# The widest probability tile of each attention step is scaled on ScalarE instead of VectorE

## The reference

```python
# fox, for each head and block of 128 queries
s = einsum('bhqd,bhkd->bhqk', qi, k) * SCALE + ci[..., None] - c[:, :, None, :]
p = masked_softmax(s, kpos[None, :] <= qpos[:, None])
o = einsum('bhqk,bkhd->bqhd', p, v)
# nsa, three such attentions (cmp, slc, win), each with a bias from a table of distances
out = sum(sigmoid(gate_logit)[..., None] * stack([o_cmp, o_slc, o_win], -2), axis=3)
```

## Time and profile before

| | us |
|---|---|
| median of 3 runs | 1925.82 |
| lowest, highest | 1923.39, 1929.86 |
| the profiled execution, its own time | 1926.27 |
| its span, first to last instruction | 1924.5 |
| busy in the span: PE, DVE, ACT | 1701.3, 1176.1, 733.3 |
| the first attention's 32 steps | from about 195 to 432 |

### The profile page before, as it was taken

How to read it: one execution, slowest core, us unless ns; L and a number is a source line. 1 busy time by engine, 2 the same in 40 slices (tenths; PEclk the granted TensorE clock), 3 DMA queues, 4 the chain that set the end, 5 groups by cost and what they waited for, 6 DMA issues and landing times.

```text
span 1924.5 us, 22173 instructions
## 1 busy us (share of the span) xinstructions
PE 1701.3 (88%) x7666; PEld 1357.5 (71%) x7666; DVE 1176.1 (61%) x1751; ACT 733.3 (38%) x1215; POOL 142.9 (7%) x162
## 2 busy tenths in 40 slices
PE   7988889989869999999779785989898699999995
PEld 5867766668747777777647553778677578888884
DVE  6465788876475565655463597778875555344354
ACT  5234766554333222222142233553332354233232
POOL 0002300000000000000200492000000000000000
PEclk9988999999979999999589797999999899999998
DMA  4236811112424444443111110002222123223232
GB/s 151 90 117 175 159 53 58 60 34 77 174 90 173 153 162 154 154 163 120 44 44 66 44 55 11 1 1 88 79 85 77 66 88 98 88 99 98 96 100 77
DMA packets 46982, 178.96 MB, mean 93 GB/s; under 512 B 6256, under 2 KB 6512, under 8 KB 44608
## 3 DMA queue, kind: packets, MB, share of 16 engines
q1 hardware_dynamic: 38304, 136.75, 21.4%
q0 software_dynamic: 8608, 41.29, 7.0%
HBM read 168.04 MB, written 4.73 MB: 90 GB/s over the span
## 4 chain that ended last, share of the span: by engine, by line
PE 56%; DVE 23%; ACT 5%; issue 5%; DMA 1%; DVEq 1%; ACTq 0%; SPq 0%
PE ps L1603 15%; PE ps L1604 14%; PE ps L1605 14%; DVE conv L1489 3%; PE ps L1864 1%; DVE rstd L1427 1%; DVE sq_acc L942 1%; DVE mod_a L1304 1%; DVE pt_lo L1452 1%; PE ps L1806 1%; DVE w_lo L931 1%; PE ps L1767 1%; PE ps L1808 1%; PE ps L1807 1%; ACT w_hi L528 1%
## 5 line engine op out<-in xcount | busy, mean ns | idle before, releaser
L1603 PE MATMUL ps<-h_hi,w_hi 128*128 128x512 f32 x1216 | 493.7, 406 | 80.2 <-DVE f_lo L1322 17.3
L1604 PE MATMUL ps<-h_lo,w_hi 128*128 128x512 f32 x1216 | 482.1, 396 | 0.0
L1605 PE MATMUL ps<-h_hi,w_lo 128*128 128x512 f32 x1216 | 481.4, 396 | 0.0
L1603 PEld LDWEIGHTS ps<-h_hi,w_hi 128*128 128x128 f32 x1216 | 233.6, 192 | 153.8 <-issue 58.6
L528 ACT ACTIVATE w_hi<-raw 128x1024 fp32r<-128x1024 f32 x198 | 208.2, 1052 | 269.3 <-DMA raw<-in_panels 262.0
L931 DVE TENSOR_TENSOR w_lo<-raw,w_hi 128x1024 fp32r<-128x1024 f32 x205 | 255.1, 1244 | 78.4 <-ACT w_hi L528 59.2
L1605 PEld LDWEIGHTS ps<-h_hi,w_lo 128*128 128x128 f32 x1216 | 233.4, 192 | 50.4
L1604 PEld LDWEIGHTS ps<-h_lo,w_hi 128*128 128x128 f32 x1216 | 234.0, 192 | 49.3 <-issue 2.9
L1605 PE MATMUL ps<-f_hi,w_lo 128*128 128x512 f32 x432 | 170.6, 395 | 0.0
L1603 PE MATMUL ps<-f_hi,w_hi 128*128 128x512 f32 x432 | 170.6, 395 | 0.0
L1604 PE MATMUL ps<-f_lo,w_hi 128*128 128x512 f32 x432 | 170.6, 395 | 0.0
(11 more groups left out here) (355 smaller groups left out, 2677.4 us busy)
## 6 DMA issues: line engine op xcount, KB each, us to landing
raw<-in_panels SPq DMA_DIRECT2D x252, 512.0 KB, 3.5
wm<-in_w_mod POOLq DMA_DIRECT2D x16, 1536.0 KB, 10.0
scratch_r<-r POOLq DMA_DIRECT2D x8, 320.0 KB, 9.4
X<-in_x SPq DMA_DIRECT2D x4, 512.0 KB, 7.7
bias<-scratch_c POOLq DMA_DIRECT2D x8, 256.0 KB, 9.1
kd<-k_hi POOLq DMA_DIRECT2D x16, 128.0 KB, 3.7
kd<-k_lo POOLq DMA_DIRECT2D x16, 128.0 KB, 5.3
bias<-scratch_r POOLq DMA_DIRECT2D x8, 256.0 KB, 2.9
```

The source lines that it names most:

```text
L1603: pe.matmul(out, w_hi[:, u, b, :], hi[:, k, :N], start=start, stop=False)
L1604: pe.matmul(out, w_hi[:, u, b, :], lo[:, k, :N], start=False, stop=False)
L1605: ins = pe.matmul(out, w_lo[:, u, b, :], hi[:, k, :N], start=False, stop=stop)
```

## The change

The multiplication of the widest tile (t = 3, 128x512) moves from DVE to ACT for the 24 steps that are fox, slc or win. DVE raises a new semaphore `factor_ready` when the factors are there, then scales three tiles (four small ones in a `cmp` step). ACT, in turn `s` behind its last `hi_turn` and ahead of the panel, the head and the bias, waits for `factor_ready` (in every turn, `cmp` too), and scales the widest tile of step `s-1`. PE's turn 0 now waits for `normed` and for `wide_normed`.

```diff
@@ scalar
+        def wide_normed(s):
+
+            if not 0 <= s < NI:
+                return
+            act.wait_ge(sem("factor_ready"), s + 1)
+            if is_big(s):
+                buf, w = scores_of(s, NT - 1)
+                f = (factor if inst[s][0] == "fox" else factor2)[:, s % 3, NT - 1:NT]
+                act.activation(buf, buf, ACT.Copy, scale=f).then_inc(sem("wide_normed"), 1)
...
             hi_turn(s - 2, 2)
             hi_turn(s - 2, 3)
+            wide_normed(s - 1)
             for g in gates_ended(s):
                 panel_hi(BASE["gate"] + g + AHEAD)
@@ vector
-            for t in range(NT):
+            dve.sem_inc(sem("factor_ready"), 1)
+            for t in range(NT if kind == "cmp" else NT - 1):
                 buf, w = scores_of(s, t)
                 last = dve.tensor_scalar(buf, buf, f[:, t:t + 1], None, ALU.mult)
             last.then_inc(sem("normed"), 1)
@@ tensor
             if j == 0:
                 pe.wait_ge(sem("normed"), s + 1)
+                pe.wait_ge(sem("wide_normed"), sum(is_big(r) for r in range(s + 1)))
```

## The result

The changed kernel takes 1943.85 us (median of 4 runs, 1943.03 to 1944.19), the kernel before 1925.58 in the same comparison (4 runs, 1923.39 to 1929.86). The ratio is 1.0093, with a 95% interval of 1.0077 to 1.0109: 18 us slower, with 1938 forecast and 1929 to 1949 as the range. The profiled execution took 1943.03, its span 1941.2, 16.7 more than before.

A forecast was written before the change was run, and what follows sets the result against it. No engine is full: PE, DVE and ACT hand work round in a ring, with ACT setting the pace in fox turns. Fox 7.1, nsa 3.9 and clock 1.5 sum to 12.5 us more, giving 1938, range 1929 to 1949.

The forecast's parts named there:

- The wait and what lies behind it: ACT stands for the factors, then scales, delaying all behind: 1.2 us in fox turns 3 to 6, fox sum 7.1.
- DVE's 0.4 us: DVE's three tiles end 0.4 us earlier in 24 steps; at most the 4.2 us PE waits for L1187 reaches the end.
- kinds a and b: Nsa turns with cmp (a) or slc (b) at the exponentials and a panel: 0.55 us later each, totals 2.25 and 1.65.
- Turn 2: Fox turn where a gate panel holds DVE: ACT's panel 2.25 us later, of which 1.1 us remain after slack.
- The nsa turns: Three kinds of turn in each of 8 heads, by cmp, slc or win at the exponentials: together 3.9 us lost.
- The clock: Longer PE gaps bring one more stretch at the lower clock in the stage: 1.5 us, from zero to four (6 us).
- The rival that named the clock: Gaps over 1 us in each turn bring the low clock four times or more: 1945 to 1953, chance 0.15.
- DVE's wait for the high part of turn 0: Sign in the fox turns: DVE's wait for `pt_hi` goes from 0.74 to near 1.9 us.
- PE's waits for the low parts: Sign: the total of PE's waits for `pt_lo` rises by several us.
- gave ACT room: Rival: ACT's wait falls into its 72.6 us of standing for PE everywhere; -3, 1923, not slower; chance 0.10.
- had DVE as the bound of the whole: Rival: DVE bounds the ring in both halves, so its 9.6 us come through: faster, 1917; chance 0.05.
- Only fox is hurt: Rival: the nsa turns absorb everything and only the fox turns lose, 7.1 - 0.8: 1932; chance 0.15.

The follow-up runs named there:

- experiment 7: The changed kernel with 20 matmuls of 128 columns more in PE's gap ahead of the third score tile of turns 3 to 9: 1941.65 us.
- experiments 1 and 2: The kernel before plus, in 1, ACT's wait for the factors without work: 1934.96 us; in 2, ACT's scaling on unread data without a wait: 1927.94 us.
- experiment 3: The kernel before with the widest tile's multiplication left out on both engines and no new wait: 1915.24 us, ratio 0.9937.
- experiment 8: The changed kernel without ACT's wait in the 8 turns where it has nothing to scale (cmp): 1941.98 us.

## Why the prediction was right, point by point

The direction and the mechanism held: the loss is ACT's wait and work ahead of everything on its list. The number, 12.5 forecast and 18 measured, was 6 us too low, nearly all of it by the clock; it stayed inside the range, which had room for a few stretches more.

How the 19.5 us of the stage divide can be read from the start of turn 0 on ACT, which lies ahead of the new wait. The one that turns the first nsa step, before and after:

```profile
271.67 0.59 ACT L688 ACTIVATE pt_hi<-ps 32x512 fp32r<-32x512 f32 x1
```

```profile
281.14 0.57 ACT L688 ACTIVATE pt_hi<-ps 32x512 fp32r<-32x512 f32 x1
```

Up to there the stage lost 11.8 us, behind it 7.7, where about 7 and 4 were forecast. In experiment 7 (282.26), with one stretch of low clock on either side as before, it's 10.7 and 5.0; less what the filling cost (2.7 to 4.1, see the clock below), the fox turns lost 6.6 to 8.0 by waits, the nsa turns 5.0.

- **The wait and what lies behind it** was the step that decided, and it held: 0.55 and 0.62 forecast, 0.50 and 0.63 in the row of L698, 1.23 a turn with the overlap of 0.10, and experiments 1 and 2 have each half by itself at 0.6.
- **DVE's 0.4 us** is right in size (0.88 instead of 1.28), and wrong in worth. I bounded it by PE's waits for L1187; experiment 3 has 10 us for it. The changed kernel doesn't collect them: in the fox turns ACT sets the pace, and where a panel is due DVE now waits for its high part, 9.9 us in 15 times over the whole stage. That wait I had reckoned with (kinds a and b, 0.55 each; the row has PE's gap grow from 0.41 to 1.00).
- **Turn 2** was priced at 1.1 us, by the slack of the products. The scores were overlooked: they need `fox_bias` and `w_lo`. From the first `gate_out` to the first head's high part it is 20.57 us before and 23.23 in experiment 7 (198.29 to 221.52), each with one stretch of low clock: 2.7 us. The wait and the scaling of turn 3 stand ahead of that high part, 1.2 of it, so turns 1 and 2 cost some 1.4.
- **The nsa turns**, 3.9 us forecast with 0.5 to 0.6 a head: four heads free of low clock in both profiles (but for the last microsecond of one) grew by 0.49 to 0.69 us, 2.5 together. The last head seems to give 2.6 us back, 14.16 instead of 16.75, but only since its high part is the one with no wait and no scaling ahead.
- **The clock** is the term that was mis-sized: one more stretch, 1.5 us. The price of a stretch was right (1.40), the number was not: seven instead of two, three of them twice as long, 35 us at the lower level instead of 8. Experiment 7 gives the price: it is 3.8 us shorter than the kernel after over the stage (249.9 instead of 253.7) and lost 2.7 to the filling, 6.5 in all, with as many stretches left as before. The stretch from 268 to 271 lies in the turns where the filling cost most, so up to 1.4 may come on top. So 6.5 to 8 of the stage's 19.5 us are the clock's, and 11.5 to 13 the waits' own, for which 11 were forecast. That the number stayed in the range is in part luck: at half speed 27 us more could have cost 13, and 1950 lies outside; they cost half of that, the long stretches since they fell where PE would have stood, which nothing in the prediction foresaw. The rival that named the clock, with four stretches and more, had 1945 to 1953, and 1944 lies just below that.
- **Signs that didn't come.** DVE's wait for the high part of turn 0 was to go from 0.74 to near 1.9 and stayed, and PE's waits for the low parts rose from 7.7 to 9.4 us, not by several. PE's delay came by the bias tile and the scores instead, 7.6 to 16.0. ACT's list, which sets the pace, is the same cause for both.
- **The rivals** that gave ACT room, or had DVE as the bound of the whole, fell: the fox pairs grow by 0.6 for either part, and change by 0.02 at most when DVE has less to do. "Only fox is hurt" fell with the row at 324.00.

That the low stretches come from the longer gaps is shown for the fox turns: both profiles with these gaps and no filling (after, experiment 8) have three from 210 to 262, and the one with the filling has none. That rests on one profiled execution of each. For nsa it is not shown: two stretches of the kernel after are missing in experiment 7 behind like gaps, and what decides there stays open. Which part of the difference of 10 us in experiment 3 is clock stays open.

## What to carry to other kernels

Before work moves to an engine because it is idle, look at when it is idle and what stands behind the new instruction on its list: ACT had 72 us of idle time in the stage, yet an operation of 0.6 us at a place where it must first wait for DVE cost those 0.5 us of waiting too, in each turn and for all that lay behind. The same operation, with its input made earlier and put into the gap where the engine stood anyway, cost nothing in the fox turns, and in the whole no more than the relief of DVE brought (ratio 1.0007). When a change adds a microsecond to PE's gaps turn after turn, as here, reckon with the lower clock several times, not once.

## What the runs showed of the hardware

- PE's granted clock fell with no gap longer than 2.5 us just ahead: the stretch from 234 to 237 follows gaps of 2.46 us and less, the one from 411 to 418 has a single gap of 0.66 in the ten microseconds ahead of it (and with the same gaps the clock stayed up in experiment 7). The first lasted 3.4 us and cost 1.40 of a turn's 10.79; the second lasted 6.8 and cost 1.2.
- More work on PE made it faster: 20 idle matmuls in the gap, 2.3 us of work, shortened a turn from 10.79 to 9.39 us; the granted clock was 1.00 there. Where the gap was shorter than they are, they cost up to 1.7.
- An activation of 128x512 with a per-row scale in place in float32 takes 0.72 us, with its successor 0.63 behind it, and the same operation on DVE 0.48. The Trainium skill, "ScalarE: Activation LUTs", What ACT_TABLE_LOAD costs, has 186 ns and 0.833 for each element of a row, and 93 for a per-partition operand, from which I estimate 706 ns. The trace agrees, with its 0.71 and 0.72.
